# Scattering the expert outputs with a plain 0/1 selection in the single-pass type, the gate values summed per slot

## What is computed

```python
def expert_choice_ffn(h, w_router, b_router, w_gate, w_up, w_down):
    cap = (EC_CAPACITY_FACTOR * S) // N_EXPERTS                     # 64
    affinity = jax.nn.softmax((h @ w_router + b_router).astype(jnp.float32), axis=-1)
    gates, idx = lax.top_k(affinity.transpose(0, 2, 1), cap)
    xin = h[bidx, idx]                                              # 64 tokens for each expert
    hid = jax.nn.silu(jnp.einsum('becd,edf->becf', xin, w_gate)) * jnp.einsum('becd,edf->becf', xin, w_up)
    y = jnp.einsum('becf,efd->becd', hid, w_down) * gates[..., None].astype(h.dtype)
    return jnp.zeros_like(h).at[bidx, idx].add(y)
```

## Time and profile before

| | us |
|---|---|
| median of 3 runs | 3067.19 |
| lowest, highest | 3066.68, 3070.63 |
| the profiled execution | 3062.95 |
| its span in the trace | 3060.8 |
| TensorE busy | 2766.7 (90%) |
| TensorE weight loads busy | 1930.3 (63%) |
| VectorE busy | 967.4 (32%) |
| ScalarE busy | 672.7 (22%) |
| POOL busy | 200.3 (7%) |
| HBM read over the span | 552.46 MB, 182 GB/s |

### The profile page before, as it was taken

One profiled execution on the slowest core, in us unless ns is written; L12 is line 12 of the kernel. 1 busy time (PEld: TensorE's weight loads), 2 busy tenths in 40 slices (PEclk: granted clock), 3 DMA queues, 4 the chain that ended last, 5 costly groups with the idle time before them and its releaser, 6 DMA issues.

```text
span 3060.8 us, 36557 instructions
## 1 busy us (share of the span) xinstructions
PE 2766.7 (90%) x15636; PEld 1930.3 (63%) x15636; DVE 967.4 (32%) x1602; ACT 672.7 (22%) x1145; POOL 200.3 (7%) x141
## 2 busy tenths in 40 slices
PE   5987767699999999999989989999999997999998
PEld 2764546343334333433368857999999784788886
DVE  3453572311111111111153252423324325433323
ACT  1312442001000100010032142322223214321222
POOL 1312110000000000000020320000000041000000
PEclk7998888699999999999989878999999996999998
DMA  7135004499999999999922111223332110133321
GB/s 252 62 137 191 17 1 167 169 416 414 406 414 420 414 408 416 417 407 413 413 51 69 39 38 42 75 76 106 93 81 71 56 59 4 56 96 90 104 81 56
DMA packets 245855, 558.39 MB, mean 182 GB/s; under 512 B 36881, under 2 KB 199059, under 8 KB 220780
## 3 DMA queue, kind: packets, MB, share of 16 engines
q1 hardware_dynamic: 234160, 548.48, 47.0%
q0 software_dynamic: 1552, 5.70, 0.6%
q10 hardware_dynamic: 10028, 2.53, 0.4%
HBM read 552.46 MB, written 4.23 MB: 182 GB/s over the span
## 4 chain that ended last, share of the span: by engine, by line
PE 84%; DVE 8%; ACT 3%; issue 2%; DMA 1%; ACTq 1%; SPq 1%; POOL 0%; DVEq 0%; PEldq 0%; POOLq 0%
PE vpsum L2079 19%; PE vpsum L1949 15%; PE apsum L2079 11%; PE vpsum L1966 7%; PE apsum L1933 4%; PE apsum L2088 3%; PE vpsum L1991 2%; PE apsum L1991 2%; PE apsum L2105 2%; PE vpsum L2105 2%; PE vpsum L1730 1%; PE vpsum L1721 1%; PE vpsum L2220 1%; PE vpsum L1806 1%; DVE arena L1244 1%
## 5 line engine op out<-in xcount | busy, mean ns | idle before, releaser
L1949 PE MATMUL vpsum<-ring,arena 128*64 128x512 f32 x2048 | 448.1, 595 | 0.8 <-ACT arena L942 0.8
L2079 PE MATMUL vpsum<-work_r,wring_r 128*128 128x264 f32 (+1 forms) x2160 | 346.2, 322 | 3.3 <-DVE work_r L1584 3.3
L2079 PE MATMUL apsum<-stream_r,wring_r 128*128 128x264 f32 (+1 forms) x2208 | 335.9, 312 | 0.0
L2079 PEld LDWEIGHTS vpsum<-work_r,wring_r 128*128 128x128 f32 x2160 | 312.2, 189 | 37.5 <-issue 5.9
L1949 PEld LDWEIGHTS vpsum<-ring,arena 128*64 128x64 f32 x2048 | 144.6, 137 | 290.3 <-issue 290.3
L2079 PEld LDWEIGHTS apsum<-stream_r,wring_r 128*128 128x128 f32 x2208 | 308.1, 192 | 22.2 <-issue 1.2
L1488 DVE TENSOR_TENSOR wring_r<-wring,wring_r 128x2048 fp32r<-128x2048 f32 (+2 forms) x97 | 200.3, 2069 | 349.1 <-ACT wring_r L992 349.1
L2079 PE MATMUL vpsum<-stream_r,wring_r 128*128 128x264 f32 (+1 forms) x1728 | 273.7, 317 | 10.5 <-DVE body L1571 10.5
L992 ACT ACTIVATE wring_r<-wring 128x2048 fp32r<-128x2048 f32 (+3 forms) x100 | 172.6, 1728 | 465.9 <-DMA wring<-w_ffn 449.7
L2079 PEld LDWEIGHTS vpsum<-stream_r,wring_r 128*128 128x128 f32 x1728 | 247.1, 192 | 31.8 <-DVE body L1571 10.9
L1966 PE MATMUL vpsum<-ring,arena 128*64 128x512 f32 x1024 | 226.8, 595 | 11.0 <-ACT arena L954 11.0
(11 more groups left out here) (423 smaller groups left out, 3110.9 us busy)
## 6 DMA issues: line engine op xcount, KB each, us to landing
ring<-w_gate SPq DMA_DIRECT2D x64, 2048.0 KB, 16.9
ring<-w_up SPq DMA_DIRECT2D x64, 2048.0 KB, 9.7
ring<-w_down SPq DMA_DIRECT2D x64, 2048.0 KB, 13.3
wring<-w_ffn SPq DMA_DIRECT2D x88, 512.0 KB, 4.7
ring<-w_ada SPq DMA_DIRECT2D x12, 2048.0 KB, 15.9
wring<-w_ffn SPq DMA_DIRECT2D x32, 704.0 KB, 4.5
ring<-w_in SPq DMA_DIRECT2D x5, 2048.0 KB, 8.9
wring<-w_in SPq DMA_DIRECT2D x10, 1024.0 KB, 5.5
```

The costliest lines, as they stand in the source:

```text
L1949: last = pe.matmul(banks[g][CAP * blk:CAP * blk + CAP, :], xin[:, 2 * r + c, :], w[:, at:at + 512], start=r + c == 0, stop=r + c == 4)
L2079: last = pe.matmul(dst, w_[:, c, col:col + P], x_.bitcast(FR), start=c == 0 and i == 0, stop=c == chunks - 1 and i == 2)
```

## The change

The selection that is transposed for the scatter is now `sel`, whose values are 0 and 1 and so are exact in fp32r; `selT_r` is written as fp32r. The gate no longer rides in it. It is summed over the tokens for each slot by four small matmuls, selg^T times a column of ones, into the first column of `XIN_BANK`; ScalarE copies the 128 sums to `slot_gate`. The result of down is multiplied by that column as it leaves PSUM: ScalarE writes the high part `ye_hi` in fp32r (a copy with a per-partition scale), VectorE the low part `ye_lo` (the product minus the high part) in fp32r. The scatter of a chunk is two fp32r matmuls, high and low, into the same bank. The first four chunks wait for the first half of `ye_lo`, the last four for the second. `ye_lo` lies on the place of `sg`, which is free by then; `arena_r` is a second name of the arena's memory for the writes in the rounded type. Nothing else changes, and no DMA does.

```diff
@@ -112,6 +112,9 @@
         with ExitStack() as names:
             ring_r = names.enter_context(nc.sbuf_tensor("ring_r", [P, NSLOT, SLOT], F32))
             first_r = names.enter_context(nc.sbuf_tensor("first_r", [P, KC * S], F32))
+        with ExitStack() as names:
+            names.enter_context(nc.sbuf_tensor("ring_room", [P, NSLOT, SLOT], F32))
+            arena_r = names.enter_context(nc.sbuf_tensor("arena_r", [P, ARENA], F32))
         with ExitStack() as names:
             wring = names.enter_context(nc.sbuf_tensor("wring", [P, NSLOT2, SLOT2], F32))
             body = names.enter_context(nc.sbuf_tensor("body", [P, BODY], F32))
@@ -315,12 +318,13 @@
         top8 = arena[0:NE, M0 + 2048:M0 + 2056]
         sel = region(M0 + 2560, TT * 2 * CAP, "p (t a c) -> p t a c", t=TT, a=2)
         selg = region(M0 + 3072, TT * 2 * CAP, "p (t a c) -> p t a c", t=TT, a=2)
-        selT = region(M0 + 3584, S, "p (a t) -> p a t", a=1)
+        selT_r = arena_r[:, M0 + 3584:M0 + 3584 + S]
         xin = region(M0 + 4096, KC * CAP, "p (c n) -> p c n", c=KC)
         sg = region(M0 + 4608, 2 * 512, "p (g f) -> p g f", g=2)
         hid = region(M0 + 5632, 2 * 512, "p (g f) -> p g f", g=2)
         hidT = region(M0 + 6656, 2 * 512, "p (g j n) -> p g j n", g=2, j=4)
-        ysb = region(M0 + 7680, D, "p (a d) -> p a d", a=1)
+        ye_hi, ye_lo = arena_r[:, M0 + 7680:M0 + 7680 + D], arena_r[:, M0 + 4608:M0 + 4608 + D]
+        slot_gate = sb("slot_gate", [P, 1])
         slots_iota = region(M0 + 8704, TT * 2 * CAP, "p (t a c) -> p t a c", t=TT, a=2)
         assert M0 + 9216 <= ARENA
 
@@ -346,7 +350,8 @@
         hT_copied = sem("hT_copied")
         xin_copied = sem("xin_copied")
         selT_copied = sem("selT_copied")
-        y_copied = sem("y_copied")
+        ye_high, ye_low = sem("ye_high"), sem("ye_low")
+        gate_summed, gate_copied = sem("gate_summed"), sem("gate_copied")
         hid_done = sem("hid_done")
         sel_done = sem("sel_done")
         acc_done = sem("acc_done")
@@ -948,14 +953,17 @@
                     act.activation(sg[:, g, :], G_BANK[g][:, :], ACT.Silu).then_inc(silu_done, 1)
                     if g == 0:
                         act.wait_ge(selT_done, e + 1)
-                        act.activation(selT[:, 0, :], SELT_BANK[:, :], ACT.Copy).then_inc(selT_copied, 1)
+                        act.activation(selT_r.bitcast(FR), SELT_BANK[:, :], ACT.Copy).then_inc(selT_copied, 1)
+                        act.wait_ge(gate_summed, e + 1)
+                        act.activation(slot_gate[:], XIN_BANK[:, 0:1], ACT.Copy).then_inc(gate_copied, 1)
                 for g in range(2):
                     act.wait_ge(hT_done, 2 * e + g + 1)
                     act.activation(arena[:, M0 + 6656 + 512 * g:M0 + 7168 + 512 * g], HT_BANK[g][:, :], ACT.Copy).then_inc(hT_copied, 1)
                 copy_tokens(e + 2)
                 act.wait_ge(down_done, 2 * e + 2)
                 for i in range(2):
-                    act.activation(ysb[:, 0, 512 * i:512 * i + 512], Y_BANK[i][:, :], ACT.Copy).then_inc(y_copied, 1)
+                    act.wait_ge(gate_copied, e + 1)
+                    act.activation(ye_hi[:, 512 * i:512 * i + 512].bitcast(FR), Y_BANK[i][:, :], ACT.Copy, scale=slot_gate[:, 0:1]).then_inc(ye_high, 1)
 
             def warm_root(n):
 
@@ -1421,6 +1429,10 @@
                     if g == 0:
                         dve.wait_ge(selT_done, e + 1)
                         select(e + 2, e + 1)
+                for i in range(2):
+                    dve.wait_ge(ye_high, 2 * e + i + 1)
+                    dve.scalar_tensor_tensor(ye_lo[:, 512 * i:512 * i + 512].bitcast(FR), Y_BANK[i][:, :], slot_gate[:, 0:1], ye_hi[:, 512 * i:512 * i + 512],
+                                             ALU.mult, ALU.subtract).then_inc(ye_low, 1)
                 for c in range(KC):
                     dve.wait_ge(scatter_done, 8 * e + c + 1)
                     dve.tensor_tensor(acc[:, c, :], acc[:, c, :], OUT_BANK[c % 4][:, :], ALU.add).then_inc(acc_done, 1)
@@ -1973,8 +1985,11 @@
                 up(e, 0, G_BANK)
                 pe.wait_ge(sel_done, 2 * e + 2)
                 for t in range(TT):
-                    last = pe.transpose(SELT_BANK[:, t * P:t * P + P], selg[:, t, :, :].rearrange("p a c -> p (a c)"), ident[:])
+                    last = pe.transpose(SELT_BANK[:, t * P:t * P + P], sel[:, t, :, :].rearrange("p a c -> p (a c)"), ident[:])
                 last.then_inc(selT_done, 1)
+                for t in range(TT):
+                    last = pe.matmul(XIN_BANK[:, 0:1], selg[:, t, :, :].rearrange("p a c -> p (a c)"), ones[:, 0:1], start=t == 0, stop=t == TT - 1)
+                last.then_inc(gate_summed, 1)
                 pe.wait_ge(acc_done, 8 * e + 1)
                 up(e, 4, U_BANK)
                 transpose_hidden(e, 0)
@@ -1983,12 +1998,15 @@
                 gather(e + 2)
                 down(e, 1)
 
-                pe.wait_ge(y_copied, 2 * e + 2)
                 pe.wait_ge(selT_copied, e + 1)
                 for c in range(KC):
+                    if c % 4 == 0:
+                        pe.wait_ge(ye_low, 2 * e + 1 + c // 4)
                     if c >= 4:
                         pe.wait_ge(acc_done, 8 * e + c - 2)
-                    pe.matmul(OUT_BANK[c % 4][:, :], ysb[:, 0, c * P:c * P + P], selT[:, 0, :], start=True, stop=True).then_inc(scatter_done, 1)
+                    for y, last_part in ((ye_hi, False), (ye_lo, True)):
+                        last = pe.matmul(OUT_BANK[c % 4][:, :], y[:, c * P:c * P + P].bitcast(FR), selT_r.bitcast(FR), start=not last_part, stop=last_part)
+                    last.then_inc(scatter_done, 1)
 
             pe.wait_ge(acc_done, 8 * NE + 1)
             pe.wait_ge(xin_copied, NE + 1)
```

## The result

| | before | after |
|---|---|---|
| median, us | 3067.61 (4 runs) | 3034.55 (4 runs) |
| lowest, highest | 3066.68, 3070.63 | 3025.48, 3043.83 |
| profiled execution, span | 3062.95, 3060.8 | 3034.09, 3032.1 |

The account below looks back on a forecast made before the run. TensorE and its stall after down were taken as the bound, the weight stream close behind. 15 x 2.77 saved less 16 x 0.93 for gate sums gave 26.7 us: 3040.5 us, range 3033 to 3052.

Parts of the forecast that it names:

- What bounds the loop: Expert loop: TensorE and its stall set the 60.88 us turn; the weight stream needs 58.8, the turn after is 59.04.
- seam: From the end of down's matmuls to the next expert's gate unit: 8.24 us before, 5.47 forecast, a gain of 2.77.
- The wait ahead of the scatter: Between down and the first scatter matmul: ScalarE's scaled copy, VectorE's low part and handoffs take 1.58 us, 1.18 before.
- The scatter at VectorE's pace: Scatter after the change: VectorE's adds, 0.61 us apart, set the pace; first add at 2.34, gate unit at 5.47.
- The gate sums: Between transposes and up unit: the new small matmuls, hidden by nothing, cost 0.93 us an expert.
- Costed at nothing: Expert loop: ScalarE's copy of the sums, the changed transposes and VectorE's delayed adds are covered and cost 0.
- The last expert: After the last down: adds end about 1.4 us sooner, but VectorE waits behind POOL that much longer; no gain counted.
- Slow handoffs: Rival at the scatter: adds stay 0.86 us apart, giving 3051.8 us; chance 0.26 together with a stream partly holding back.
- a bound stream: Rival in the expert loop: the weight stream already sets the pace, so about 3064 us, no change; chance 0.05.
- two instructions a matmul: Rival at the scatter: the new matmuls are not single-pass, giving 3197 us; the slower cases together had 0.05.
- The fall of the clock: Rival at the stall after down: TensorE's clock falls, giving 3093 or 3205 us; the slower cases together had 0.05.
- Does the stream hold?: Down's weight loads: they land 2.1 us before they are wanted, a reserve that stays while the turn is above 58.8.

Follow-up runs that it names:

- e6: The changed kernel with the loads of down's units halved (result not the reference's): median 3031.97 us in one run, turn 59.01 us.
- e4: The changed kernel with the gate sums moved behind the up units, where TensorE waits anyway: median 3026.32 us, 0.9878 of the kernel before.
- e7: The changed kernel without the low part, one scatter matmul for each chunk: median 3027.87 us in one run, turns 57.9 to 60.4 us.
- e8: e7 with the loads of down's units halved (result not the reference's): median 3015.83 us in one run, turn 57.93 us.
- e2: The changed kernel with the gate sums done twice: median 3047.01 us, 0.9942 of the kernel before, turn 59.91 us.
- e1: The changed kernel measured again, unchanged: median 3033.21 us, 0.9892 of the kernel before, turn 59.01 us.
- e9: The kernel before measured again, unchanged, against itself: median 3064.98 us, ratio 1.0004, turn 60.88 us.
- e5: e4 with the loads of down's units halved (result not the reference's): median 3022.81 us, 0.9862 of the kernel before, turn 58.23 us.
- e3: The changed kernel with the scatter back to 8 fp32 matmuls and no low part: median 3061.56 us, 0.9998 of the kernel before.

## Why the prediction was right, step by step

- **What bounds the loop.** TensorE and its seam were said to set the pace, with the stream 0.24 us behind. e6 shows the first, e4 and e7 the second: the turn can't stay below about 58.7. The reading of the earlier trace rows (428 GB/s, 58.8 us an expert) held to 0.1 us, where the share of 0.98 in the earlier trace rows read alone would have said that the stream was the bound already.
- **The wait ahead of the scatter**, 1.58 forecast and 1.66 measured. ScalarE's copy took 0.683 (0.69 said), the low part 0.746 (0.75 said). Mis-sized is one handoff: from VectorE's end (807.34 + 0.75 = 808.09) to the matmul's start are 0.15 us, not 0.05. The second half is hidden, as was said: both low parts are done at 807.34 + 1.41 = 808.75, ahead of the first add at 808.97.
- **The scatter at VectorE's pace.** First add at 2.39 behind down (2.34 said), pitch 0.60 (0.61 said), gate unit at 5.59 (5.47 said). The gain in the seam is 2.65, not 2.77. e8 confirms the mechanism, that the adds pace it: with half the matmuls they stay 0.60 apart.
- **The gate sums**, 0.93 forecast, 0.79 measured (e2). The 0.12 an instruction of the earlier trace rows was 0.113 here (0.90 for 8), and the rest is the 0.11 shorter step behind the transposes. This and the seam's error cancel nearly: 2.65 - 0.79 = 1.86 against 1.84, so the turn of 59.04 came out at 59.01. That the loop's 27.2 us meet the 26.7 forecast so closely is therefore luck in part: 15 x 0.12 = 1.8 us too much was counted in the seam, and 16 x 0.14 = 2.2 us too much for the sums.
- **Costed at nothing**: ScalarE's copy of the sums, the transposes, the adds that end later. No wait at the up units, or for `slot_gate`, is among TensorE's three waits above.
- **The last expert.** Nothing was counted, and nothing came. The tail after, of POOL and VectorE, as the earlier trace rows:

```profile
1517.99 14.01 POOL L702 TENSOR_TENSOR wring_r<-wring,wring_r 128x2048 fp32r<-128x2048 f32 x3 [959.88 <-ACT wring_r L1000]
...
1522.62 13.93 DVE L1493 SCALAR_TENSOR_TENSOR body<-arena,mod 128x512 f32<-128x512 f32 x8
```

VectorE starts them sooner and is 2.0 us longer at it (11.93 before). From the end of down to the second block's first projections are 34.57 us (to 1549.29), and 34.49 before (to 1581.51).
- **The rivals.** Slow handoffs would have shown as a pitch of 0.86; a bound stream as a turn of 60.88 and waits on ring; two instructions a matmul as a seam of 15.4. All three are refuted by rows above. The fall of the clock, which was to begin at 1.84 us a turn of work at half the clock, has 0 us of it in the loop. The psum-queue depth-cycling of the Trainium skill (TensorE: Matmul & The Clock Gate, section A second HAM failure mode: psum-queue depth-cycling) did not come about at this seam, though TensorE goes through four banks there and idles 1.66 us (before, 1.19).
- **Does the stream hold?** The text said that a gain of 2.5 an expert would use up the reserve after some five experts. e4's gain is 60.88 - 58.23 = 2.65, and its first long turn is the sixth.

**The median** fell by 33.1 where the trace gives 27.2 and the forecast was 26.7; 3034.55 lies 1.5 us inside the range. The further 6 us, which the forecast did not have at all, must lie outside the loop, as its turns repeat to 0.01 us. The profiled executions differ by 28.9, but that of before was 4.7 under its median and that of after 0.5. Beside e1 the medians differ by 33.3 with an interval of 27 to 40, and e6, with the same turn as after, stands 30.8 under its kernel before. The kernel before itself had medians between 3062.8 and 3067.6, and the part outside the loop varied from 2136.9 to 2150.1 among traces.

One place of this variation can be read from the traces: the same stretch of the second block's work, some 85 us behind the last down, in before, in after and in e1 (the last three numbers are the granted clock, the DMA share and GB/s):

```profile
1632.53:1873.84 241.31, 211.54 (x1316) 168.55 (x1315) 89.26 (x184) 70.85 (x187) 43.21 (x24) 0.82 0.12 38
1600.26:1841.45 241.19, 211.42 (x1315) 168.44 (x1314) 89.26 (x184) 70.86 (x187) 43.19 (x24) 0.82 0.12 38
1611.92:1846.17 234.25, 203.95 (x1315) 162.70 (x1314) 89.30 (x184) 70.90 (x187) 43.20 (x24) 0.85 0.12 39
```

It takes 241 us at a mean granted clock of 0.82 or 0.83 in before, e9, after, e5 and e7, and 234 us at 0.85 in e1, e2, e3, e4, e6 and e8. The 7 us are TensorE's time at the lower clock, and the code there is the same in all. The start of the loop varies too: ScalarE's first copy of down began at 633.89 before and at 629.58 after, and at 641.13 in e1.

Whether some of the 6 us belong to the change stays open. Both traces of the kernel before have the long form, but so have three of the nine with the change in them. In after and e1 to e4 the medians are lower than the turns give by 5.9 to 12.5 us, most in e3; in e5 to e8, which have four runs or one each, it is -0.3 to 3.6. That five of five are on one side speaks for a part that goes with the change, though e1 to e4 are held against the same runs of the kernel before. e9's 2146.1 outside the loop lies in the range expected and under the 2151 of its rival, but a second trace of a kernel that can take two forms doesn't settle it.

e8's turn was expected at 57.6 and came at 57.93. Its scatter starts 0.88 behind down where 0.77 was expected, and from there to the gate unit are 3.64 us where 3.4 were expected; the pace of the adds was as expected.

## What to carry to other kernels

When two resources are both near full, look for what each does in the stall of the other: here the DMA queue ran dry in TensorE's seam, so its 0.98 was an effect of the seam and not the bound. After a change to a faster matmul type, recount the chain in the engine that empties the banks, since the pace can pass to it as it did here: 3.2 us freed on TensorE gave 2.65. And put new small work on the bound engine where it waits already: the same eight instructions cost 0.79 us a turn between two full stages and nothing in a 0.89 us gap, until the weights become the floor. By its loop, 5.2 us shorter than e1's, e4 is the fastest of the kernels here that leave nothing out (0.9878, though its interval overlaps e1's).

## What was not expected of the hardware

**A short wait can halve TensorE's clock where a longer one doesn't.** In the changed kernel TensorE idles 1.66 us at each seam, between full stages, and the clock stays at 1.00. In e4's sixth turn it waits 1.07 us for weights, behind the sums and transposes. The timeline there, and four windows over it:

```profile
960.59 1.46 PE L1962 MATMUL vpsum<-ring,arena 128*64 128x512 f32 x6
961.98 1.05 PE L1994 MATMUL apsum<-ones,arena 128*128 128x1 f32 x8
962.94 0.75 PE L1969 MATMUL apsum<-ident,arena 128*128 128x128 f32 x4
964.76 8.78 PE L1979 MATMUL vpsum<-ring,arena 128*64 128x512 f32 x32 [1.07 <-DMA ring<-w_down]
```

```profile
964.00:966.00 2.00, 1.24 (x4) 0.56 (x6) 0.89 (x2) 0.32 (x1) 0.00 (x0) 0.72 1.04 442
966.00:968.00 2.00, 2.00 (x6) 0.61 (x4) 0.00 (x0) 0.00 (x0) 0.00 (x0) 0.50 1.04 442
968.00:970.00 2.00, 2.00 (x12) 0.88 (x10) 0.00 (x0) 0.00 (x0) 0.00 (x0) 0.93 0.96 410
970.00:972.00 2.00, 2.00 (x12) 0.78 (x10) 0.00 (x0) 0.00 (x0) 0.00 (x0) 1.00 1.00 426
```

The clock falls to 0.50 (1.2 GHz), and the half of down takes 8.78 us where 7.09 is its time. A wait 0.38 us longer than the usual 0.69 thus costs 0.38 + 1.69 = 2.07, the 2.08 by which that turn (60.31) exceeds 58.23. The turns of 60.23 and 60.42 have the same, with waits of 1.00 and 1.19 us; the turn of 58.54 has a wait of 0.99 and keeps its clock. e7, whose sums stand elsewhere, has only the transposes between VectorE's wait and that for the weights. Here are two of its seven waits for weights, the first in a turn of 60.43, the second in one of 58.72:

```profile
960.24 8.78 PE L1974 MATMUL vpsum<-ring,arena 128*64 128x512 f32 x32 [1.54 <-DMA ring<-w_down]
1195.14 7.09 PE L1974 MATMUL vpsum<-ring,arena 128*64 128x512 f32 x32 [1.52 <-DMA ring<-w_down]
```

Its two waits of 1.54 us took the clock to 0.50, and those of 0.91 to 1.52 us left it at 1.00. So the clock fell in a wait of 1.00 us behind the sums and transposes, and stayed in one of 1.52 behind a wait of 0.89 and the transposes, and in one of 1.66 behind full 512-column matmuls. This speaks for the work ahead of the idle time as a cause beside its length, but no run changed that work alone, and waits of 0.99 and 1.00 us behind the same work came out differently in e4, so the account isn't complete. It makes e4's last step toward the stream dearer than the wait itself, and the rival of the clock, refuted at the seam, real one stage away.

**One core streams its weights at 428 or 429 GB/s for 756 us.** So say ten slices in a row (the 10th to the 19th, 75.6 us each) on e4's page:

```profile
GB/s 255 63 125 205 19 1 139 140 421 429 428 429 428 429 429 428 429 428 429 400 53 56 47 17 57 83 73 103 90 86 58 56 63 1 56 107 82 112 76 57
```

The Trainium skill, HBM Reference, section Specifications (TRN2), gives about 425 GB/s for a core that streams alone, and these slices agree within 1%; the 358 GB/s weighed ahead of the result is, by that section, the share of each core when both of a pair stream.
